# Head norms of a two-layer block: head sums in two rounded passes, the low half formed on GpSimd, and two causal products moved

## The reference

```
y  = o * rsqrt(mean(o*o, axis=-1) + EPS)          # per head, 128 values per token
uA = head_rms_norm(oA, hg_norm_g) * silu(hz)
uB = head_rms_norm(oB, ret_norm_g) * silu(rz)
m  = sigmoid(ga)*uA + sigmoid(gb)*uB;  x = x + gate*(m @ w_out)
```

## Time and profile before

| what | value |
| --- | --- |
| three runs | 1680.17, 1681.71, 1682.74 us (median 1681.71) |
| the profiled execution | 1681.25 us, its span 1679.4 us |
| mean granted TensorE clock | 0.991 |
| TensorE matmul busy | 1631.0 us (97%) |
| VectorE, ScalarE, GpSimd busy | 813.3, 730.9, 715.6 us |

### The profile page before, as it was taken

How to read it: one execution, slowest core, us unless ns; L and a number is a source line. 1 busy time by engine, 2 the same in 40 slices (tenths; PEclk the granted TensorE clock), 3 DMA queues, 4 the chain that set the end, 5 groups by cost and what they waited for, 6 DMA issues and landing times.

```text
span 1679.4 us, 22093 instructions
## 1 busy us (share of the span) xinstructions
PE 1631.0 (97%) x8056; PEld 1325.5 (79%) x8056; DVE 813.3 (48%) x1348; ACT 730.9 (44%) x1027; POOL 715.6 (43%) x303
## 2 busy tenths in 40 slices
PE   6999999999999999989999999999999999999997
PEld 4887887887887778548888888888787888888885
DVE  6685575575575858965221221235565221121123
ACT  4454454454454654555431222245565442222232
POOL 1443444444344437914544444444214444444442
PEclk9999999999999999999999999999999999999999
DMA  9322321322322346422323233232112233223231
GB/s 375 127 88 66 122 88 64 116 89 70 112 87 75 128 76 163 131 88 88 113 99 102 88 100 100 88 108 92 64 52 87 89 100 100 87 100 100 88 100 63
DMA packets 52323, 170.97 MB, mean 102 GB/s; under 512 B 5771, under 2 KB 10412, under 8 KB 51756
## 3 DMA queue, kind: packets, MB, share of 16 engines
q1 hardware_dynamic: 46000, 157.82, 28.0%
q10 hardware_dynamic: 6268, 12.39, 3.1%
HBM read 161.63 MB, written 5.24 MB: 99 GB/s over the span
## 4 chain that ended last, share of the span: by engine, by line
PE 62%; issue 2%; DVE 2%; ACT 2%; POOL 2%; SPq 1%; DMA 0%; DVEq 0%; ACTq 0%; POOLq 0%
PE gps L1456 18%; PE gps L1457 18%; PE gps L1458 18%; POOL conv L519 1%; SPq L461 1%; PE gps L1748 1%; PE aps L1813 1%; PE aps L1823 1%; PE gps L1835 1%; POOL w_lo L491 1%; PE gps L1483 1%; PE gps L1484 0%; PE aps L1511 0%; ACT scores L904 0%; PE gps L1504 0%
## 5 line engine op out<-in xcount | busy, mean ns | idle before, releaser
L491 POOL TENSOR_TENSOR w_lo<-w_raw,w_hi 128x1024 fp32r<-128x1024 f32 x260 | 665.4, 2562 | 925.7 <-ACT w_hi L557 925.5
L1456 PE MATMUL gps<-xa_hi,w_hi 128*128 128x512 f32 x1128 | 450.3, 399 | 5.4 <-DVE xa_lo L1002 5.2
L1458 PE MATMUL gps<-xa_hi,w_lo 128*128 128x512 f32 x1128 | 439.8, 390 | 0.0
L1457 PE MATMUL gps<-xa_lo,w_hi 128*128 128x512 f32 x1128 | 439.6, 390 | 0.0
L557 ACT CAST w_hi<-w_raw 128x1024 fp32r<-128x1024 f32 x260 | 271.1, 1044 | 217.9 <-PE gps L1458 136.2
L1456 PE MATMUL gps<-xb_hi,w_hi 128*128 128x512 f32 x736 | 288.3, 392 | 3.0 <-POOL w_lo L491 1.7
L1458 PE MATMUL gps<-xb_hi,w_lo 128*128 128x512 f32 x736 | 286.5, 389 | 0.0
L1457 PE MATMUL gps<-xb_lo,w_hi 128*128 128x512 f32 x736 | 286.4, 389 | 0.0
L1456 PEld LDWEIGHTS gps<-xa_hi,w_hi 128*128 128x128 f32 x1128 | 212.1, 188 | 55.6 <-issue 6.5
L1457 PEld LDWEIGHTS gps<-xa_lo,w_hi 128*128 128x128 f32 x1128 | 212.2, 188 | 44.7 <-issue 3.1
L1458 PEld LDWEIGHTS gps<-xa_hi,w_lo 128*128 128x128 f32 x1128 | 211.9, 188 | 44.9
(11 more groups left out here) (253 smaller groups left out, 1884.8 us busy)
## 6 DMA issues: line engine op xcount, KB each, us to landing
w_raw<-weights_dram SPq DMA_DIRECT2D x268, 512.0 KB, 3.3
ada_w<-ada_in_dram SPq DMA_DIRECT2D x8, 1024.0 KB, 17.2
gates<-ret_tab_dram ACTq DMA_DIRECT2D x4, 1024.0 KB, 6.2
spread<-glu SPq DMA_DIRECT2D x48, 67.5 KB, 2.0
rel_scratch_dram<-rel_rows ACTq DMA_DIRECT2D x1, 3072.0 KB, 34.5
x<-x_turned_dram SPq DMA_DIRECT2D x2, 1024.0 KB, 8.4
res<-xT_dram ACTq DMA_DIRECT2D x1, 2048.0 KB, 8.5
bias<-rel_scratch_dram ACTq DMA_DIRECT2D x1, 2048.0 KB, 10.9
```

The source lines that it names most:

```text
L491: TT(w_lo[:, j, :], w_raw[:, j, :], w_hi[:, j, :].bitcast(F32), ALU.subtract).then_inc(lo_ready[j], 1)
L1456: mm(gps[:, j, :], w_hi[:, j, w], x[0][:, k, :], start=k == 0, stop=False)
L1457: mm(gps[:, j, :], w_hi[:, j, w], x[1][:, k, :], start=False, stop=False)
L1458: last = mm(gps[:, j, :], w_lo[:, j, w], x[0][:, k, :], start=False, stop=k == blocks - 1)
```

## The change

The ones matrix is written as a rounded (float32r) tile and read as float32 everywhere else. Behind each square ScalarE copies it, rounded, into `osq_hi`. GpSimd forms `osq_lo`, the square less its rounded part, at places between its `w_low` that a table gives. TensorE's head sum becomes two rounded passes, the second of which waits for GpSimd. On VectorE `causal(2)` and `causal(3)` come in front of the gate product of chunk 12. Some small tiles change their place in memory, and `reset` is halved.

```
+HEAD_LOW_AFTER = {17: ((0, 0),), 18: ((0, 1),), 21: ((1, 0), (1, 1))}

 # GpSimd
             with pool.Fori(0, PAIRS) as p:
+                def head_low(e, r):
+                    pool.wait_ge(osq_high, p * 4 + (2 * e + r + 1))
+                    TT(osq_lo[:, r, :], hbuf[:, 2 + r, :], osq_hi[:, r, :].bitcast(F32), ALU.subtract).then_inc(osq_low, 1)
                 for c in LOW_ORDER:
                     w_low(p * (PAIR_CHUNKS // SLOTS) + (START["pairs"] + c // SLOTS), c % SLOTS)
+                    for e, r in HEAD_LOW_AFTER.get(c, ()):
+                        head_low(e, r)

 # ScalarE
                 def head_square(e, r):
                     nc.scalar.activation(hbuf[:, 2 + r, :], bank(U_AV[e][r]), ACT.Square).then_inc(osq_ready, 1)
+                    act.wait_ge(osq_ready, p * 4 + (2 * e + r + 1))
+                    nc.scalar.copy(osq_hi[:, r, :], hbuf[:, 2 + r, :]).then_inc(osq_high, 1)

 # VectorE
-            nc.vector.memset(ones[:], 1.0)
+            own.done(nc.vector.memset(lnv[:, 0:P], 1.0))
+            TT(ones_r[:], lnv[:, 0:P], lnv[:, 0:P], ALU.mult)
...
                 causal(0)
                 causal(1)
-                z_gate(12, 0, 0, "hg_norm_g")
                 causal(2)
                 causal(3)
+                z_gate(12, 0, 0, "hg_norm_g")
                 z_gate(13, 1, 0, "hg_norm_g")

 # TensorE
                 def head_sum(e, r):
                     u = U_NORM[e][r]
-                    pe.wait_ge(osq_ready, p * 4 + (2 * e + r + 1))
-                    mm(bank(u), ones[:], hbuf[:, 2 + r, :], start=True, stop=True).then_inc(bank_full[u % 4], 1)
+                    pe.wait_ge(osq_high, p * 4 + (2 * e + r + 1))
+                    b = bank(u)
+                    mm(b, ones_r[:], osq_hi[:, r, :], start=True, stop=False)
+                    pe.wait_ge(osq_low, p * 4 + (2 * e + r + 1))
+                    mm(b, ones_r[:], osq_lo[:, r, :], start=False, stop=True).then_inc(bank_full[u % 4], 1)
```

More of the change, by code:

```diff
@@ L193, in program @@
         vec = sb("vec", [P, VECS])
-        ones = sb("ones", [P, P])
+        ones_r = sb("ones_r", [P, P], F32R)
+        ones = ones_r[:].bitcast(F32)
         ident = sb("ident", [P, P])
@@ L205, in program @@
         sink_neg = sb("sink_neg", [P, AH])
[L206 to L210, removed]
         first = ExitStack()
-        reset = sb("reset", [P, T], where=first)
+        reset = sb("reset", [P, 2 * P], where=first)
         tri = sb("tri", [P, T + P], where=first)
@@ L243, in program @@
         at_r = sb("at_r", [P, 2, 10 * P], where=first)
+        osq_hi = sb("osq_hi", [P, 2, T], F32R, where=first)
+        osq_lo = sb("osq_lo", [P, 2, T], F32R, where=first)
         first.close()
@@ L269, in program @@
         pT = sb("pT", [P, 2, 2 * NT - 1, P], where=attn_mem)
+        row_min = sb("row_min", [P, 2, NT], where=attn_mem)
+        row_all = sb("row_all", [P, 2, NT], where=attn_mem)
+        row_sum = sb("row_sum", [P, 2, NT], where=attn_mem)
+        row_inv = sb("row_inv", [P, 2, NT], where=attn_mem)
+        sink_exp = sb("sink_exp", [P, 2, NT], where=attn_mem)
         attn_mem.close()
@@ L331, in program @@
         hnorm = sem("hnorm")
+        osq_high = sem("osq_high")
+        osq_low = sem("osq_low")
         gate_sig = sem("gate_sig")
```

## The result

The changed kernel takes 1701.56 us (median of four runs, 1701.1 to 1702.11) against 1680.94 for the kernel before (four runs, 1679.45 to 1682.74): a ratio of 1.0123 [1.011, 1.0135], 20.6 us more. The forecast was 1689.0 and "slower"; the direction is right, the size is outside the range of 1685 to 1695.

A forecast was written before the change was run, and what follows sets the result against it. TensorE, busy for 97% of 1679.4 us, was taken as the bound. Head 0 gives 0, head 1 loses 3 x 2.0 + 1.35 = 7.35 us on 1681.25: 1688.6, as a median 1689.0, range 1685.0 to 1695.0.

The forecast's parts named there:

- Other edits: ScalarE's copies, VectorE's start and GpSimd's later low parts: almost no cost, 0.3 us once if VectorE's start is uncovered.
- the forecast for all the rest: Head stage: 2.0 us lost in each of three pairs and 1.35 in the last, 7.35 us more.
- Head 1: Head 1's sums: TensorE's second passes wait for GpSimd's subtractions behind chunk 21's low part; a pair loses 2.0 us.
- Head 0: Head 0's sums: waits for GpSimd's subtractions behind chunks 17 and 18 eat all gains; 0 per pair.
- rival (d): Head sums: rounded passes as slow as float32 ones, 0.43 each; 1692 us; chance 0.07 together with anything else slow.
- rival (b): Head 0, chunk 17's low part: GpSimd gets the port before VectorE's series; 1680.4 us, not slower; chance 0.1.
- Rival (a): Behind head 1's waits: the clock falls too, 1.7 us each; two falls 1692.4, four 1695.8; chance 0.28.
- the last pair and the end: Behind the last pair TensorE idles until L750's copies; 0.65 of the 2.0 us is absorbed, leaving 1.35.

The follow-up runs named there:

- b_moved: The kernel before with xb_hi and what follows it 160 B lower, nothing else changed: 1694.95 us, ratio 1.0085.
- b_causal_first: The kernel before with only the two causal products put in front of the gate product of chunk 12: 1674.43 us, ratio 0.9961.

## Why the prediction was right and wrong

**The step that failed.** The sum had no term for the small tiles that change their place, although the diff shows it. It prices "Other edits" engine by engine, as work and as order, and a tile's place is neither. It cost 13.4 us (1701.56 less 1688.18), two thirds of the result: the matmuls on `xb` went from 0.2267 to 0.233 apart. Why a place is slow stays open. With `xb` where it was, the kernel is at 1688.18, 7.0 us over its session's 1681.19; the forecast for all the rest was 7.35, and it is close by luck (below). No rival held this: all four lay in the head stage.

**Head 1: right.** TensorE's sums in the second pair, timeline of the kernel after:

```profile
290.06 0.40 PE L1688 MATMUL aps<-osq_hi,ones_r 128*128 128x512 f32 x1
291.90 0.50 PE L1690 MATMUL aps<-osq_lo,ones_r 128*128 128x512 f32 x1 [1.44 <-POOL osq_lo L507]
292.23 0.39 PE L1688 MATMUL aps<-osq_hi,ones_r 128*128 128x512 f32 x1
293.61 0.51 PE L1690 MATMUL aps<-osq_lo,ones_r 128*128 128x512 f32 x1 [0.98 <-POOL osq_lo L507]
293.95 0.39 PE L1472 MATMUL gps<-xa_hi,w_hi 128*128 128x512 f32 x1
```

The second passes (`osq_lo`) follow 1.84 and 1.38 behind the first; 1.82 and 1.5 were predicted (288.56 to 290.38, then 290.6 to 292.1). VectorE's gate product (L1127 before, L1143 now) gets in between the two subtractions. GpSimd, then VectorE:

```profile
288.22 2.39 POOL L497 TENSOR_TENSOR w_lo<-w_raw,w_hi 128x1024 fp32r<-128x1024 f32 x1 [13.63 <-ACT w_hi L570]
290.56 2.99 POOL L507 TENSOR_TENSOR osq_lo<-hbuf,osq_hi 128x512 fp32r<-128x512 f32 x2
```

```profile
290.89 1.50 DVE L1143 TENSOR_TENSOR gates<-gates,sq 128x512 f32<-128x512 f32 x1 [9.38 <-ACT sq L738]
```

The two subtractions end 2.99 after they began, of which 2 x 1.29 is work, so the gate product cost them 0.41 (0.45 predicted); it took 1.50 instead of 0.69 itself. From the first pass to the next dense matmul it is 3.89 where it was 1.73 (2 x 0.865): 2.16 lost, 2.0 predicted. The measured value was the right choice over the whole 0.69 that the rule of the Trainium skill ("SBUF — State Buffer", section "SBUF: two separate sides") gave.

**Head 0: the mechanism was wrong.** Predicted were waits of 1.7 and 0.4 and a gain of nothing. Timeline of TensorE after:

```profile
259.25 0.40 PE L1688 MATMUL aps<-osq_hi,ones_r 128*128 128x512 f32 x1
259.49 0.39 PE L1690 MATMUL aps<-osq_lo,ones_r 128*128 128x512 f32 x1
259.72 0.39 PE L1472 MATMUL gps<-xa_hi,w_hi 128*128 128x512 f32 x1
...
262.48 0.40 PE L1688 MATMUL aps<-osq_hi,ones_r 128*128 128x512 f32 x1
263.20 0.50 PE L1690 MATMUL aps<-osq_lo,ones_r 128*128 128x512 f32 x1 [0.33 <-POOL osq_lo L507]
...
268.81 0.39 PE L1474 MATMUL gps<-xa_hi,w_lo 128*128 128x512 f32 x1
269.38 0.35 PE L1609 MATMUL aps<-packed 128*128 128x128 f32 x1 [0.19 <-DVE unit L1132]
```

`attend(0, 0)` starts 0.23 behind the dense matmul (248.47 to 248.70), as predicted. The passes are 0.24 and 0.23 apart, which puts an end to rival (d). But the first sum has no wait, and the second has one of 0.5. GpSimd shows why:

```profile
254.28 2.35 POOL L497 TENSOR_TENSOR w_lo<-w_raw,w_hi 128x1024 fp32r<-128x1024 f32 x1 [0.18 <-ACT w_hi L570]
256.59 1.49 POOL L507 TENSOR_TENSOR osq_lo<-hbuf,osq_hi 128x512 fp32r<-128x512 f32 x1
```

The low part of chunk 17 takes 2.35, not 5.78: GpSimd gets in behind the first of VectorE's decay products, which started at 252.94. That has the effect of rival (b), though not by (b)'s way: the series is late, the request isn't early. The race for the port was turned round some 14 us earlier, at chunk 14, where the prediction didn't look; VectorE has been 2.2 us late since. So head 0 gains what the passes and the causal products give, less two smaller waits. In a pair without a fall of the clock: 1.35 + 4 x 0.40 = 2.95 gained; lost are 0.5 at the second sum, 0.35 at L1609 and 2.96 at head 1 (the 2.16 and the 2 x 0.40 that its passes save). That is a loss of 0.86 us, of which head 0 gains 1.3 and head 1 loses 2.16. The third pair's length went from 127.1 to 127.8.

**Rival (a) happened in three pairs.** The windows of pairs from token stage to token stage: the first and third pair before, then the first and third after, the stretches behind head 1 of the second and of the fourth, and the start of the output projection:

```profile
94.90:221.70 126.80, 125.46 (x679) 105.17 (x680) 82.78 (x143) 65.04 (x78) 54.22 (x18) 1.00 0.28 92
348.40:475.50 127.10, 125.80 (x683) 105.32 (x682) 82.69 (x141) 65.04 (x78) 50.84 (x18) 1.00 0.29 96
```

```profile
94.70:224.30 129.60, 126.34 (x679) 106.17 (x680) 88.42 (x143) 67.60 (x82) 54.17 (x22) 0.99 0.27 90
353.70:481.50 127.80, 124.85 (x684) 105.14 (x682) 88.28 (x141) 67.59 (x82) 54.12 (x22) 1.00 0.27 90
294.50:297.90 3.40, 3.40 (x10) 2.62 (x9) 2.85 (x3) 3.35 (x5) 1.58 (x1) 0.50 0.19 46
550.75:554.15 3.40, 3.39 (x8) 2.69 (x9) 2.75 (x2) 2.67 (x4) 2.47 (x1) 0.53 0.00 0
559.60:563.30 3.70, 3.70 (x15) 2.09 (x15) 3.42 (x5) 3.59 (x7) 2.65 (x2) 1.00 0.92 304
```

Behind the waits of head 1 the granted clock was about 0.50, that is 1.2 GHz, for 3.4 us in the first, second and fourth pair, 1.7 us each. The first three pairs grew by 2.8, 2.7 (126.7 to 129.4) and 0.7 us, so by 1.1, 1.0 and 0.7 without the falls. The rest of the 8.0, 1.8, lies in the last pair and the end (1.35 predicted): 0.86 and the third fall, less 0.6, because the wait at the end went from 1.97 to 1.38 (0.65 predicted).

So the 7.35 for the head stage came out close (8.0) because two errors met. Head 0 was taken for 1.3 us too little in each pair, 5.2 in all, and three falls of the clock, 5.1, were left to a rival. That is luck, and not a proof of the head stage's sum.

## What to carry to other kernels

Price a tile's place too: when a diff moves the tiles that a hot instruction reads, even by 32 bytes, compare the spacing of that instruction from start to start before and after, and pad the tile back by the difference before judging the rest. Where two engines share a port, look for the first place at which their order can turn round, not only at the one that TensorE waits for; and form a small operand ahead of the next long item of an engine's queue, not behind it, when another engine waits for it (here 14 us, over a third of it by the clock). A wait taken away by reordering one engine can come back elsewhere at a higher price, here 4 to 5 us.

## What the hardware showed that was not expected

- Rounded matmuls of 128x512 are 0.2267 us apart with `xb` in its old place or a multiple of 256 B from it (256, 512 and 2048 tried), and 0.233 apart at 32, 64, 128 or 160 B from it: 3%, 11.6 to 13.8 us over the program. `xb_hi` may have lain a multiple of 256 B from `w_hi` too: the sizes of the tiles between them give that if the 4 B of `eps_col` take up 32, which no run shows. Whether the address itself counts or the distance between the two operands is open; no kernel moved the weights.
- GpSimd's request in the midst of a series of VectorE's two-operand products is sometimes served at once (2.36 us) and sometimes at the end of the series (3.70, 3.82), for the same instruction in the same execution. Nine kernels with the first block's tiles in the old place keep the late outcome in all 36 pairs; every kernel with them in the new place has the early one in some pairs or all. What decides it is open. The Trainium skill, "SBUF — State Buffer", section "SBUF: two separate sides", has the exclusion, and the trace agrees (5.78 against 2.37); the page speaks of one instruction that is waited out, and here it was the rest of a series.
- Two starts of TensorE that come 1.84 and 1.38 us late, with two passes between them, were followed by 3.4 us at 1.2 GHz in the first, second and fourth pair and not in the third, with the same gaps. The wait of 2.0 at the start of the output projection had such a stretch behind it in the kernel before and none in b_moved and b_causal_first.
